# A decoder layer on one core: the delta rule takes q unnormalised, its decay differences come from rows spread by DMA, and the tile order is chosen anew

## The chip, the cores and the metric

The kernel runs on one core of one Trainium2 chip. TensorE (PE) multiplies, VectorE (DVE), ScalarE (ACT) and GpSimd (POOL) do the elementwise work, and the SyncE queue (SP) issues every DMA. The metric is the device time of one execution in microseconds, as the median of three runs. All data are float32. A projection is computed as three products of "hi" and "lo" halves, so each of its K-steps is three matmuls.

## What is computed

The layer mixes 512 tokens of width 1024 by three branches (differential attention, gated DeltaNet, cross-attention into 256 memory tokens), merges them by gates, and ends with a squared-ReLU MLP. The change is in the DeltaNet branch. Cut to that:

```python
q = chunk(l2norm(q.astype(f32)) * dk ** -0.5)
k = chunk(l2norm(k.astype(f32)))
G = jnp.cumsum(g, axis=-1)
decay = jnp.exp(jnp.where(causal, G[..., :, None] - G[..., None, :], -jnp.inf))
lower = jnp.where(strict, jnp.einsum('bhnid,bhnjd->bhnij', k_beta, k) * decay, 0.0)
sol = lax.linalg.triangular_solve(lower + jnp.eye(C), rhs, left_side=True, lower=True, unit_diagonal=True)
intra = jnp.where(causal, jnp.einsum('bhnid,bhnjd->bhnij', q, k) * decay, 0.0)
q_dec = q * jnp.exp(G)[..., None]
...
v_new = u_c - jnp.einsum('bhcd,bhde->bhce', w_c, state)
o = jnp.einsum('bhcd,bhde->bhce', qd, state) + jnp.einsum('bhij,bhje->bhie', a_c, v_new)
...
y_b = rms_norm(o_dn, dn_norm_g) * jax.nn.silu(dn_z)
```

The output of each head is RMS-normalised over its 128 values, so a factor common to a whole row of o (that of q's own norm) falls out, except for the epsilon that is added under the root.

## The kernel before

Work is cut into weight tiles of 128 output columns. A mixing tile takes its weights from a 512 KB load (`w_raw`, three buffers), ACT rounds them to `w_hi`, DVE makes `w_lo`, and PE runs 8 K-steps of three matmuls into one of two accumulator banks (`main_part`, L1749 to L1751: 24 matmuls of 512 columns, or of 256 for the 16 memory tiles `mk` and `mv`). ACT then empties the bank (`evacuate`). PE may start tile t once the evacuation of tile t-2 is done. There are 104 mixing tiles; after them come the branch, output and MLP tiles, which the change leaves alone.

Between pieces of these tiles PE runs two other chains, each a list of steps that use one PSUM area: attention (`ps_a`) and the delta rule (`ps_d`). The delta rule handles the 8 heads in 4 pairs; one pair is 8 blocks of 128 x 128 (2 heads x 4 chunks of 128 tokens). The steps of a pair, in PE's order: `dv`, `dk`, `dq` transpose the convolved v, k, q to rows of tokens; `dE` multiplies a masked copy of the decays (made on POOL in `ET`) by a triangle of ones, and ACT turns the product into `ET = exp(differences)`; `dkT`, `dkb` transpose k and beta k; `dL` forms the triangular matrix; `T1` and the steps `Za`, `Wb`, `Z5`, `W5`, `Zl`, `Wl` invert it in 32 x 32 pieces; `dqT` and `dqd` transpose the normalised q, without and with its decay; `dA` forms q k^T; `dU`, `dW` and the chunk steps `sa`, `sb` run the recurrence; `dO` transposes the result. Behind `dq` DVE squares, sums, takes a root and scales q (`scale_by_norm`, L1493 to L1501).

The order on every engine is not written out: `plan_order` places each step when its inputs are due, from a table of durations, over the tile sequence `ORDER`. Each engine's queue is then strictly in order, SP's too. `decay` (PE L1925, ACT L1180) makes the exponentials of the running decays once, for all heads, and signals `g_exp`. SP's queue also carries the three steps of the attention bias (`bias`): step 1 (L833) spreads 8 rows to a 1.5 MB scratch tensor, `bias_rows`, step 2 (L837) reads `strip` from it. A gate tile is evacuated into the single buffer `gate_st`, halved and shifted on POOL (L960), and stored by SP (L853); the evacuation of the next gate tile waits until that store has landed (`g_out`, L1091).

## Time and profile before

| | |
|---|---|
| median of 3 runs | 1385.65 us (1385.17 to 1386.16) |
| the profiled execution | 1388.61 us, of which the span from its first to its last instruction is 1386.8 us |
| granted PE clock, mean | 0.994 |
| PE, DVE, ACT, POOL busy | 1363.1, 775.9, 483.7, 190.3 us |
| mixing tiles | until 819.8 us |
| matmuls on PE in the trace | 10588 |

The page gives the busy time of each engine, the chain of work that ended last, and groups of instructions with their mean duration and the idle time before them. Matmuls are pipelined: the duration of one (0.39 us for 512 columns) is longer than the distance to the next one's start (0.23 us). What a matmul costs PE is therefore read from starts in the timeline.

### The profile page before, as it was taken

How to read it: one execution, taken by the hardware profiler on the slowest of the kernel's cores; microseconds unless marked ns; L12 is line 12 of the kernel's file. 1: busy time of each engine (PE TensorE's matmuls, PEld its weight loads, DVE VectorE, ACT ScalarE, POOL GpSimd, SP SyncE). 2: the span in 40 equal slices, each digit the busy share in tenths (PEclk: the TensorE clock that was granted, in tenths of full speed). 3: DMA queues.
4: the chain of work that ended last, by engine and by line, in shares of the span. 5: the costliest groups of instructions: out<-in, count | busy, mean ns of one | idle time of the engine just before them, and what ended most of it. 6: DMA issues, size and time to landing. Idle time of an engine off the chain costs nothing.

```text
span 1386.8 us, 24640 instructions
## 1 busy us (share of the span) xinstructions
PE 1363.1 (98%) x10588; PEld 1133.9 (82%) x10588; DVE 775.9 (56%) x1281; ACT 483.7 (35%) x782; POOL 190.3 (14%) x138
## 2 busy tenths in 40 slices
PE   8999999999999999999999999999989999999998
PEld 8689887887888877887888888888988888888886
DVE  6796327844865957769554534554366522355332
ACT  5244433433534434444334221113533212222220
POOL 1112000020000200002101232232202200022010
PEclk9999999999999999999999999999999999999998
DMA  5144322212123222222222466644323323232221
GB/s 213 61 175 139 109 69 91 81 65 78 55 76 99 81 66 63 77 87 89 70 66 96 148 209 195 185 145 154 125 66 119 92 93 102 94 92 91 91 61 61
DMA packets 46435, 143.15 MB, mean 103 GB/s; under 512 B 4944, under 2 KB 7416, under 8 KB 46328
## 3 DMA queue, kind: packets, MB, share of 16 engines
q1 hardware_dynamic: 46328, 141.59, 31.9%
q8 instruction: 84, 1.38, 0.4%
q14 instruction: 23, 0.19, 0.0%
HBM read 126.88 MB, written 16.27 MB: 103 GB/s over the span
## 4 chain that ended last, share of the span: by engine, by line
PE 89%; DVE 7%; ACT 1%; issue 1%; DMA 1%; SPq 0%; DVEq 0%; ACTq 0%
PE acc L1749 24%; PE acc L1751 23%; PE acc L1750 23%; PE ps_d L1903 2%; PE ps_a L1824 2%; PE ps_a L1835 1%; PE ps_d L1865 1%; DVE w_lo L1314 1%; DVE conv_y L1416 1%; PE ps_a L1814 1%; PE ps_a L1803 1%; PE ps_d L1875 1%; PE ps_d L1879 1%; PE ps_d L1881 1%; PE ps_a L1830 1%
## 5 line engine op out<-in xcount | busy, mean ns | idle before, releaser
L1749 PE MATMUL acc<-n_hi,w_hi 128*128 128x512 f32 (+1 forms) x888 | 356.4, 401 | 2.0 <-ACT conv_x L1085 1.4
L1751 PE MATMUL acc<-n_hi,w_lo 128*128 128x512 f32 (+1 forms) x888 | 343.2, 386 | 0.0
L1750 PE MATMUL acc<-n_lo,w_hi 128*128 128x512 f32 (+1 forms) x888 | 342.7, 386 | 0.0
L1013 ACT CAST w_hi<-w_raw 128x1024 fp32r<-128x1024 f32 x172 | 180.4, 1049 | 386.8 <-PE acc L1751 386.2
L1314 DVE TENSOR_TENSOR w_lo<-w_raw,w_hi 128x1024 fp32r<-128x1024 f32 x172 | 237.3, 1384 | 117.0 <-ACT w_hi L1013 116.2
L1749 PEld LDWEIGHTS acc<-n_hi,w_hi 128*128 128x128 f32 x888 | 167.3, 188 | 37.8 <-issue 4.6
L1751 PEld LDWEIGHTS acc<-n_hi,w_lo 128*128 128x128 f32 x888 | 167.1, 188 | 36.3
L1750 PEld LDWEIGHTS acc<-n_lo,w_hi 128*128 128x128 f32 x888 | 167.6, 189 | 30.8 <-issue 0.5
L960 POOL TENSOR_SCALAR gate_st<-gate_st 128x512 f32<-128x512 f32 x24 | 24.7, 1028 | 468.5 <-ACT gate_st L1092 468.4
L1751 PE MATMUL acc<-y_hi,w_lo 128*128 128x512 f32 x192 | 76.0, 396 | 0.0
L1749 PE MATMUL acc<-y_hi,w_hi 128*128 128x512 f32 x192 | 76.0, 396 | 0.0
L1750 PE MATMUL acc<-y_lo,w_hi 128*128 128x512 f32 x192 | 76.0, 396 | 0.0
L1001 POOL TENSOR_TENSOR h_lo<-sq,h_hi 128x512 fp32r<-128x512 f32 x32 | 41.4, 1292 | 239.9 <-DVE h_hi L1671 239.9
L1259 ACT ACTIVATE sq<-relu 128x512 f32<-128x512 f32 x32 | 20.2, 632 | 123.6 <-DVE relu L1669 123.6
L1749 PE MATMUL acc<-h_hi,w_hi 128*128 128x512 f32 x152 | 60.0, 395 | 0.0
L1750 PE MATMUL acc<-h_lo,w_hi 128*128 128x512 f32 x152 | 60.0, 395 | 0.0
L1751 PE MATMUL acc<-h_hi,w_lo 128*128 128x512 f32 x152 | 60.0, 395 | 0.0
L1416 DVE SCALAR_TENSOR_TENSOR conv_y<-conv_x,par,conv_y 128x512 f32<-128x512 f32 x72 | 57.4, 797 | 2.6
L1314 DVE TENSOR_TENSOR wx_lo<-w_raw,wx_hi 128x1024 fp32r<-128x1024 f32 x28 | 45.5, 1636 | 11.5 <-ACT wx_hi L1013 11.5
L1013 ACT CAST wx_hi<-w_raw 128x1024 fp32r<-128x1024 f32 x28 | 29.2, 1041 | 45.5 <-PE acc L1751 45.1
L1751 PEld LDWEIGHTS acc<-y_hi,w_lo 128*128 128x128 f32 x192 | 36.2, 188 | 8.7
L1750 PEld LDWEIGHTS acc<-y_lo,w_hi 128*128 128x128 f32 x192 | 36.2, 188 | 8.7
(359 smaller groups left out, 2339.8 us busy)
## 6 DMA issues: line engine op xcount, KB each, us to landing
w_raw<-weights SPq DMA_DIRECT2D x200, 512.0 KB, 3.7
gate_scratch<-gate_st SPq DMA_DIRECT2D x24, 256.0 KB, 2.8
g_in<-gate_scratch SPq DMA_DIRECT2D x24, 256.0 KB, 4.0
y_raw<-y_scratch SPq DMA_DIRECT2D x16, 256.0 KB, 3.8
x_tok<-x SPq DMA_DIRECT2D x4, 512.0 KB, 5.5
y_scratch<-y_st SPq DMA_DIRECT2D x4, 512.0 KB, 3.0
y_scratch<-d_ET SPq DMA_DIRECT2D x4, 512.0 KB, 3.8
y_scratch<-y_st SPq DMA_DIRECT2D x8, 256.0 KB, 2.5
```

Of the source, the lines that this page charges most:

```text
L960: nc.gpsimd.tensor_scalar(gate_st[:], gate_st[:], 0.5, 0.5, ALU.mult, ALU.add).then_inc(gs_ready, 1)
L1001: nc.gpsimd.tensor_tensor(h_lo[:, f % 16], sq[:, f % 2], h_hi[:, f % 16].bitcast(F32), ALU.subtract).then_inc(hl_ok, 1)
L1013: nc.scalar.copy(hi_of_tile(t), w_raw[:, t % RAW]).then_inc(hi_ready, 1)
L1259: nc.scalar.activation(sq[:, f % 2], relu[:, f % 2], ACT.Square).then_inc(sq_ok, 1)
L1314: V_.tensor_tensor(lo_of_tile(t), w_raw[:, t % RAW], hi_of_tile(t).bitcast(F32), ALU.subtract).then_inc(lo_ready, 1)
L1416: ins = V_.scalar_tensor_tensor(out=y, in0=conv_x[:, n % 2, j:j + S], scalar=par[:, col + j:col + j + 1], in1=y, op0=ALU.mult, op1=ALU.add)
L1749: mm(bank, wh, hi_of(k), start=start and k == 0, stop=False)
L1750: mm(bank, wh, lo_of(k), start=False, stop=False)
L1751: last = mm(bank, wl, hi_of(k), start=False, stop=stop and k == KT - 1)
L1803: last = mm(ps_a[:, s // 2, (s % 2) * MEM:(s % 2 + 1) * MEM], cq_T[:, h % 2, dt, s * P:(s + 1) * P], mk_T[:, 2 * h + dt], start=dt == 0, s ...
L1824: last = mm(ps[:, col:col + (q + 1) * P], qkv_T[rows_m, h % 2, 0, q * P:(q + 1) * P], qkv_T[rows_m, h % 2, 1, 0:(q + 1) * P], start=True, ...
L1903: last = mm(dst[m], a[:, m], b[:, m], start=True, stop=True)
```

## The change

1. **Raw q.** `dq` still transposes q, but ACT writes only its squares (`U`), and copies the convolved q as it is to `QT`, which needs no transposition. DVE sums the squares to `q_eps`, the epsilon for the output's norm. The norm of q, `dqT` and `dqd` go, on PE, ACT and DVE. The decay that was multiplied into q is now multiplied into the product: in `sb` the product of q and the state goes to a bank of its own, and DVE adds it, scaled, to what ACT has copied (two instructions for each chunk but the first, which wait for ACT).
2. **Spread rows.** `decay` gets a fourth product, the running decays as 32 rows, which ACT copies into `ET`; it also writes the running decays over `gdec`. SP stores the rows (`store_rows`, 16 KB) and reads them back for each pair into all 128 partitions (`spread_rows`, 512 KB as 1024 pieces of 512 bytes). POOL subtracts where it multiplied. ACT, within `dq`, waits for POOL and applies Relu and Exp. `dE` goes from PE.
3. **Tile order.** `ORDER` is another, and all engines' orders follow from it and from the changed table of durations.

```diff
@@ plan
-ORDER = [("conv", 0), ("z", 0), ("gate", 1), ("mem", 0), ("cq", 0), ("gate", 1), ("cq", 1), ("conv", 1),
...
+ORDER = [("conv", 0), ("gate", 2), ("z", 0), ("mem", 0), ("cq", 0), ("cq", 1), ("conv", 1), ("cq", 2),
...
-        out += [(k, p, 0) for k in ("dv", "dk", "dq", "dE", "dkT", "dkb", "dL", "T1", "dqT", "dA", "dqd")]
+        out += [(k, p, 0) for k in ("dv", "dk", "dq", "dkT", "dkb", "dL", "T1", "dA")]
...
+    add("SP", "rows", ("rows_out", 0), 0.1, [("AT", 2)])
+    for p in range(HB // 2):
+        add("SP", "rows", ("rows", p), 0.1, [("OUT", "yb", d_idx[("dO", p - 1, 0)]) if p else ("OUT", "rows_out", 0)])
@@ sync
+            def store_rows(n):
+
+                sp.wait_ge(g_exp, 1)
+                sp.dma_start(row_dram, ET[0:HB * ST, 0]).then_inc(rows_out, 16)
+
+            def spread_rows(p):
+
+                if p:
+                    sp.wait_ge(yb_out, 16 * p)
+                else:
+                    sp.wait_ge(rows_out, 16)
+                sp.dma_start(ET[:], bass.AP(tensor=row_dram.tensor, offset=row_dram.offset + 8 * p * row_dram.ap[0][0],
+                                            ap=[[0, P], [row_dram.ap[0][0], 8], [1, P]])).then_inc(rows_in, 16)
@@ gpsimd
-                    if p:
-                        pool.wait_ge(yb_out, 16 * p)
-                    last = nc.gpsimd.tensor_tensor(ET[:], over(cst[:, C_AFTER, :], 8),
-                                                   along(flat(gdec[:, heads]), P), ALU.mult)
+                    pool.wait_ge(rows_in, 16 * (p + 1))
+                    last = nc.gpsimd.tensor_tensor(ET[:], along(flat(gdec[:, heads]), P), ET[:], ALU.subtract)
@@ scalar
-                if kind == "dE":
-                    last = nc.scalar.activation(flat(ET[:]), two(ps_d), ACT.Exp)
+                if kind == "dq":
+                    nc.scalar.activation(flat(U[:]), two(ps_d), ACT.Square)
+                    nc.scalar.copy(flat(QT[:]), conv_o[:, 0].rearrange("p a s -> p (a s)"))
+                    act.wait_ge(d_pool, dP[d_idx[("dk", p, 0)] + 1])
+                    nc.scalar.activation(flat(ET[:]), flat(ET[:]), ACT.Relu).then_inc(ach, 1)
+                    act.wait_ge(ach, p + 1)
+                    last = nc.scalar.activation(flat(ET[:]), flat(ET[:]), ACT.Exp, scale=-1.0)
...
+                nc.scalar.copy(flat(gdec[:]), ps_d[:, 2, 0:32])
+                nc.scalar.copy(ET[0:HB * ST, 0], ps_d[0:HB * ST, 2, P:2 * P]).then_inc(g_exp, 1)
@@ vector
-                    last = scale_by_norm(Q, 1.0, 4 * EPS, P ** -0.5)
+                    dve.wait_ge(g_exp, 1)
+                    link(V_.reduce_sum(q_eps, U[:], AX_X))
+                    last = V_.tensor_scalar(q_eps, q_eps, 4 * EPS, EPS * P, ALU.add, ALU.mult)
...
-                elif kind == "dqT":
-                    dve.wait_ge(g_exp, 1)
-                    last = V_.tensor_tensor(Q[:], Q[:], along(flat(e_in[:, heads]), P), ALU.mult)
...
+                    dve.wait_ge(d_act, dA[i + 1])
+                    if c:
+                        for hh in range(2):
+                            last = V_.scalar_tensor_tensor(out=O[:, 4 * hh + c], in0=ps_d[:, 2, hh * P:(hh + 1) * P],
+                                                           scalar=e_in[:, 2 * p + hh, c:c + 1], in1=O[:, 4 * hh + c],
+                                                           op0=ALU.mult, op1=ALU.add)
@@ tensor
-                elif kind in ("dqT", "dqd", "dkT", "dkb", "dO"):
-                    src = {"dqT": Q, "dqd": Q, "dkT": K, "dkb": KB, "dO": O}[kind]
+                elif kind in ("dkT", "dkb", "dO"):
+                    src = {"dkT": K, "dkb": KB, "dO": O}[kind]
...
-                elif kind == "dE":
-                    for m in range(8):
-                        last = mm(dst[m], ET[:, m], cst[:, C_UPTO, :], start=True, stop=True)
...
-                            mm(o_ps, QDT[:, 4 * hh + c], state[:, hh], start=True, stop=False)
-                        mm(o_ps, AT[:, 4 * hh + c], vn, start=c == 0, stop=True)
+                            mm(ps_d[:, 2, hh * P:(hh + 1) * P], QT[:, 4 * hh + c], state[:, hh], start=True, stop=True)
+                        mm(o_ps, AT[:, 4 * hh + c], vn, start=True, stop=True)
...
+                mm(ps_d[0:HB * ST, 2, P:2 * P], flat(gdec[:]), cst[:, C_UPTO, :], start=True, stop=True).then_inc(g_mm, 1)
```

The first place is PE where pair 0 enters its inversion: `dqd` (L1865 on `d_Q`) ahead of the first `Za` (L1875). Before:

```order
L1751 MATMUL acc<-m_hi,w_lo 128x256
L1865 MATMUL ps_d<-cst,d_Q 128x128 x8
L1875 MATMUL ps_d<-d_TT,d_SCR 32x32 x32
L1749 MATMUL acc<-m_hi,w_hi 128x256
L1750 MATMUL acc<-m_lo,w_hi 128x256
```

The same place now (L1901 is `Za`, L1780 to L1782 are the tile's products):

```order
L1782 MATMUL acc<-m_hi,w_lo 128x256
L1901 MATMUL ps_d<-d_TT,d_SCR 32x32 x32
L1780 MATMUL acc<-m_hi,w_hi 128x256
L1781 MATMUL acc<-m_lo,w_hi 128x256
```

The eight transpositions are gone and nothing stands in their place; the same holds for `dqT` and `dE`, in each of the four pairs.

The second place is SP's queue from the last load ahead of the spread bias to the load of `strip`. Before (L833 is `bias` step 1, L837 step 2, L853 the store of the first gate tile):

```order
L815 DMA w_raw<-weights 128x1024 x4
L833 DMA bias_rows<-bias_scratch 1024x1x384
L815 DMA w_raw<-weights 128x1024 x3
L837 DMA strip<-bias_rows 128x8x256
L853 DMA gate_scratch<-gate_st 128x512
L815 DMA w_raw<-weights 128x1024 x20
```

Now (L881 stores the rows, L889 spreads those of pair 0, L840 is `bias` step 1, L860 stores the gate tiles 6 and 7, L844 is `bias` step 2):

```order
L822 DMA w_raw<-weights 128x1024 x4
L881 DMA y_scratch<-d_ET 32x128
L889 DMA d_ET<-y_scratch 128x8x128
L840 DMA bias_rows<-bias_scratch 1024x1x384
L822 DMA w_raw<-weights 128x1024
L860 DMA gate_scratch<-gate_st 128x512
L822 DMA w_raw<-weights 128x1024
L860 DMA gate_scratch<-gate_st 128x512
L822 DMA w_raw<-weights 128x1024
L844 DMA strip<-bias_rows 128x8x256
```

The 1.5 MB transfer now stands behind two row transfers, and ahead of the first gate tile's store, with one load between.

The third place is ACT's queue over the same time. Before, from the copy of k (L1173, step `dk`) to that of q (step `dq`):

```order
L1173 COPY d_K<-ps_d 128x1024
L1099 ACTIVATE conv_x<-conv_y 128x512
L1106 ACTIVATE z_t<-zs 128x512
L1013 CAST w_hi<-w_raw 128x1024
L1087 COPY zs<-acc 128x512
L1013 CAST w_hi<-w_raw 128x1024
L1092 ACTIVATE gate_st<-acc 128x512
L1013 CAST w_hi<-w_raw 128x1024
L1068 COPY mk_T<-acc 128x256
L1173 COPY d_Q<-ps_d 128x1024
```

Now, from the first gate tile's evacuation (L1112) to the end of `dq` (L1171 to L1176) and the next tile's:

```order
L1112 ACTIVATE gate_st<-acc 128x512
L1198 COPY d_K<-ps_d 128x1024
L1119 ACTIVATE conv_x<-conv_y 128x512
L1033 CAST w_hi<-w_raw 128x1024
L1112 ACTIVATE gate_st<-acc 128x512
L1033 CAST w_hi<-w_raw 128x1024
L1107 COPY zs<-acc 128x512
L1126 ACTIVATE z_t<-zs 128x512
L1171 ACTIVATE d_U<-ps_d 128x1024
L1172 COPY d_QT<-conv_o 128x1024
L1174 ACTIVATE d_ET<-d_ET 128x1024
L1176 ACTIVATE d_ET<-d_ET 128x1024
```

The second gate tile (tile 7) is evacuated here, ahead of the casts and copies of the tiles behind it, where before there was one gate tile in this stretch; and `dq` is four full passes in a row.

## Rows read from the trace of the kernel before

**Rows 1.** The page, busy time, share of the span and instructions of each engine.

```profile
PE 1363.1 (98%) x10588; PEld 1133.9 (82%) x10588; DVE 775.9 (56%) x1281; ACT 483.7 (35%) x782; POOL 190.3 (14%) x138
PE 89%; DVE 7%; ACT 1%; issue 1%; DMA 1%; SPq 0%; DVEq 0%; ACTq 0%
```

**Rows 2.** PE by stretch: stretch in us, its length, PE busy (instructions), clock, DMA.

```profile
40.00:100.00 60.00, 55.37 (x285) 1.00 0.36 122
100.00:820.00 720.00, 717.82 (x7408) 1.00 0.29 90
```

**Rows 3.** Waits of PE: who waited for whom, us in total, times, longest.

```profile
PE ps_d L1879 <- issue: 1.5, 1, 1.5
PE acc L1749 <- ACT conv_x L1085: 1.4, 1, 1.4
PE ps_d L1860 <- DVE conv_o L1430: 1.2, 1, 1.2
PE ps_d L1860 <- DVE d_V L1518: 0.7, 1, 0.7
PE ps_d L1875 <- DVE d_KBT L1525: 0.6, 1, 0.6
```

**Rows 4.** Timeline of PE at `dE` of pair 1: start us, us, instruction.

```profile
273.56 1.95 PE L1868 MATMUL ps_d<-cst,d_ET 128*128 128x128 f32 x16
275.26 0.48 PE L1749 MATMUL acc<-n_hi,w_hi 128*128 128x512 f32 x1
275.58 0.39 PE L1750 MATMUL acc<-n_lo,w_hi 128*128 128x512 f32 x1
275.81 0.39 PE L1751 MATMUL acc<-n_hi,w_lo 128*128 128x512 f32 x1
```

**Rows 5.** Timeline of PE at `dqT` of pair 0.

```profile
119.64 1.03 PE L1865 MATMUL ps_d<-cst,d_Q 128*128 128x128 f32 x8
120.43 0.36 PE L1749 MATMUL acc<-m_hi,w_hi 128*128 128x256 f32 x1
120.63 0.28 PE L1750 MATMUL acc<-m_lo,w_hi 128*128 128x256 f32 x1
```

**Rows 6.** Timeline of ACT at `decay`, start us, us, instruction.

```profile
75.90 0.20 ACT L1180 ACTIVATE e_all<-ps_d 128x32 f32<-128x32 f32 x1
```

**Rows 7.** Timeline of SP: issues of the bias, loads and the first gate store.

```profile
72.82 0.75 SPq L833 DMA_DIRECT2D bias_rows<-bias_scratch  x1
83.33 9.94 SPq L815 DMA_DIRECT2D w_raw<-weights  x3
93.79 0.58 SPq L853 DMA_DIRECT2D gate_scratch<-gate_st  x1
```

**Rows 8.** DMA from 74 to 86 us: GB/s moved, in 40 equal slices of 0.3 us.

```profile
GB/s 259 259 341 273 217 188 189 205 195 205 205 205 195 195 200 200 205 205 200 200 205 205 200 195 195 205 200 205 205 195 184 118 15 0 55 96 191 273 382 423
```

**Rows 9.** DMA issues from 60 to 100 us: KB each, median us to landing.

```profile
strip<-bias_rows SPq DMA_DIRECT2D x1, 1024.0 KB, 6.2
gate_scratch<-gate_st SPq DMA_DIRECT2D x1, 256.0 KB, 6.4
```

**Rows 10.** Landing times of all gate stores and reloads, then of all weight loads.

```profile
DMA to landing us min/median/max: 2.0/3.9/6.4
DMA to landing us min/median/max: 3.3/3.7/12.1
```

**Rows 11.** Timeline of PE where tile 9 begins, and at `dO` of pair 3.

```profile
89.85 0.28 PE L1749 MATMUL acc<-m_hi,w_hi 128*128 128x256 f32 x1
...
791.02 1.03 PE L1865 MATMUL ps_d<-cst,d_LT 128*128 128x128 f32 x8
...
819.77 0.40 PE L1749 MATMUL acc<-y_hi,w_hi 128*128 128x512 f32 x1
```

**Rows 12.** Groups of DVE and ACT: form xcount, busy us, mean ns.

```profile
L1549 DVE SCALAR_TENSOR_TENSOR state<-state,e_all,ps_d 128x128 f32<-128x128 f32 x24 | 7.2, 343 | 11.8 <-PE ps_d L1916 11.6
L1173 ACT COPY d_Q<-ps_d 128x1024 f32<-128x1024 f32 x8 | 8.1, 1016 | 20.2 <-PE ps_d L1903 13.1 <-PE ps_d L1860 7.1
```

More of the change, by code:

```diff
@@ L124, in vector_before @@
     kind, p, c = step
-    return {"dq": ("dv", p, 0), "dE": ("dv", p, 0), "dkT": ("dk", p, 0), "dkb": ("dk", p, 0), "dL": ("dk", p, 0),
-            "T1": ("dL", p, 0), "dqT": ("dL", p, 0), "dA": ("dL", p, 0), "dqd": ("dqT", p, 0)}.get(kind)
+    return {"dq": ("dv", p, 0), "dkT": ("dk", p, 0), "dkb": ("dk", p, 0), "dL": ("dk", p, 0),
+            "T1": ("dL", p, 0), "dA": ("dL", p, 0)}.get(kind)
 def scalar_before(step):
@@ L257, in plan_order @@
                 add("ACT", "fin", ("fin", t), 0.65, [("DVE", "conv", t)])
-                add("DVE", "fin", ("fin", t), 0.75, [("ACT", "fin", t)] + ([("PE", "delta", d_idx[free])] if free else []))
+                add("DVE", "fin", ("fin", t), 0.75, [("ACT", "fin", t)] + ([("ACT" if tiles[t][0] == "dq" else "PE", "delta", d_idx[free])]
+                                                                  if free else []))
             else:
@@ L273, in plan_order @@
             deps.append(("POOL", "delta", d_idx[pool_before(s)]))
-        if kind == "dqd":
-            deps.append(("DVE", "at", p))
         if kind in ("dq", "dk", "dv"):
@@ L280, in plan_order @@
         if "A" in PARTS[kind]:
-            add("ACT", "delta", ("delta", i), ACT_US.get(kind, 1.05), [mm, ("DVE", "delta", i) if kind == "dL" else ("POOL", "delta", d_idx[("dA", p, 0)]) if kind == "W5" else None])
+            add("ACT", "delta", ("delta", i), ACT_US.get(kind, 1.05), [mm, ("DVE", "delta", i) if kind == "dL" else ("POOL", "delta", d_idx[("dA", p, 0)]) if kind == "W5" else
+                                                                ("POOL", "delta", d_idx[("dk", p, 0)]) if kind == "dq" else None])
         if "D" in PARTS[kind]:
@@ L295, in plan_order @@
                 deps.append(("DVE", "at", p))
-            if kind == "dk" and p:
-                deps.append(("OUT", "yb", d_idx[("dO", p - 1, 0)]))
+            if kind == "dk":
+                deps.append(("OUT", "rows", p))
             add("POOL", "delta", ("delta", i), POOL_US[kind], deps)
@@ L333, in plan_order @@
             "DVE": ("lo", "delta", "attn", "conv", "fin", "finz", "pre"), "POOL": ("delta", "gate", "pre"),
-            "SP": ("load", "gate", "y", "yb", "bias", "pre")}
-    landing = {"load": 3.7, "gate": 2.4, "y": 3.4, "yb": 3.4, "pre": 3.8, "bias": 0.0, "load_gate": 3.8}
+            "SP": ("load", "gate", "y", "yb", "rows", "bias", "pre")}
+    landing = {"load": 3.7, "gate": 2.4, "y": 3.4, "yb": 3.4, "pre": 3.8, "bias": 0.0, "load_gate": 3.8, "rows_out": 2.4, "rows": 4.5}
     order = {e: [] for e in rank}
@@ L498, in build @@
         sd_ = sb_in(dl)
-        names = ["Q", "SCR", "K", "KB", "V", "QT", "QDT", "KTT", "KBT", "ET", "LT", "AT", "TT"]
+        names = ["U", "SCR", "K", "KB", "V", "TF", "QT", "KTT", "KBT", "ET", "LT", "AT", "TT"]
         B = {n: sd_("d_" + n, [P, 8, P]) for n in names}
-        Q, SCR, K, KB, V, QT, QDT, KTT, KBT, ET, LT, AT, TT = (B[n] for n in names)
-        TF, U, WT, O = QT, Q, SCR, LT
+        U, SCR, K, KB, V, TF, QT, KTT, KBT, ET, LT, AT, TT = (B[n] for n in names)
+        WT, O = SCR, LT
         HP = (slice(0, P // 2), slice(P // 2, P))
@@ L628, in build @@
         g_exp = sem("g_exp")
+        rows_out = sem("rows_out")
+        rows_in = sem("rows_in")
         f_mm = sem("f_mm")
@@ L879, in _ @@
             sp_work = {"load": load, "bias": bias, "gate": store_gate, "y": store_attn, "yb": store_delta,
+                       "rows_out": store_rows, "rows": spread_rows,
                        "pre": reload, "load_gate": load_gate}
@@ L1171, in delta @@
                 else:
-                    dst = {"dq": Q, "dk": K, "dqT": QT, "dqd": QDT, "dkT": KTT, "dkb": KBT, "dU": U, "dW": WT}[kind]
+                    dst = {"dk": K, "dkT": KTT, "dkb": KBT, "dU": U, "dW": WT}[kind]
                     last = nc.scalar.copy(flat(dst[:]), two(ps_d))
@@ L1179, in decay @@
                 for m, dst in enumerate((e_in, e_tail, e_all)):
-                    last = nc.scalar.activation(flat(dst[:]), ps_d[:, 2, m * 32:(m + 1) * 32], ACT.Exp)
-                last.then_inc(g_exp, 1)
+                    nc.scalar.activation(flat(dst[:]), ps_d[:, 2, m * 32:(m + 1) * 32], ACT.Exp)
+                nc.scalar.copy(flat(gdec[:]), ps_d[:, 2, 0:32])
+                nc.scalar.copy(ET[0:HB * ST, 0], ps_d[0:HB * ST, 2, P:2 * P]).then_inc(g_exp, 1)
             def ba_copy():
@@ L1853, in delta @@
                     pe.wait_ge(d_pool, dP[d_idx[pool_before(DELTA[i])] + 1])
-                if kind == "dqd":
-                    pe.wait_ge(at_ready, p + 1)
                 dst = [ps_d[:, m // 4, (m % 4) * P:(m % 4 + 1) * P] for m in range(8)]
```

37 lines of the change are left out of this document (19 added, 18 removed), and 2 rows, old and new, of the table PARTS.

## The prediction

> **What bounds the kernel now.** I read the busy shares and the chain of waits first: PE is busy for 98% of the span and holds 89% of the chain that ended last, while DVE is busy for 56%, ACT for 35%, POOL for 14% [rows 1]. PE by stretch comes next. From 100 us to 820 us, where the delta rule and the attention run between pieces of the weight tiles, PE stands idle for 2.2 of 720 us; from 40 us to 100 us for 4.6 of 60 [rows 2]. Its granted clock is full (1.00) in both. So the mixing stage is a queue of PE work without holes, and its length is the sum of what stands in that queue. The delta chain itself does not set the end: its last step, `dO` of pair 3, starts at 791.0 us, and gate tiles fill PE until 819.8 us [rows 11]. What a removed matmul saves is therefore its own time on PE, and a changed wait costs only what it leaves PE idle. The waits of PE in this stage are five short ones, 0.6 to 1.5 us [rows 3].
>
> **What PE loses.** `dE`: its 16 instructions take from 273.56 to 275.26 us, 1.70 us, and the tile's first matmul behind them needs 0.32 us to the next start where 0.23 us is usual, so 1.79 us a pair [rows 4], 7.2 us for four. `dqT`: 0.79 us, and 0.20 us against 0.12 us behind it, 0.87 us a pair [rows 5], 3.5 us for four. `dqd` is the same eight transpositions; it stands right ahead of `Za`, which keeps the restart, so 0.79 us a pair, 3.2 us for four. `decay` gains one product of 128 columns, an eighth of a `dE`: 0.2 us. In `sb` the product with the state goes to its own bank; the number and shape of matmuls stay the same. PE's work falls by 7.2 + 3.5 + 3.2 - 0.2 = **13.7 us**.
>
> **What the other engines gain and lose; it costs nothing as long as PE's queue covers it.** ACT did four passes of 128 x 1024 a pair for these steps (q, ET, QT, QDT), each about 1.02 us [rows 12], and now does four others (Square, copy, Relu, Exp), but in one row, 4.2 us at the same pace with casts counted a little dearer. They are hidden by what PE has queued between `dq` and the next step of its chain, `dkT`: the least is in pair 0, 12 matmuls of 512 columns and 24 of 256, 12 x 0.23 + 24 x 0.12 = 5.6 us. Without that cover it would be up to 4.2 us a pair. Behind these passes on ACT are queued the casts and the evacuations; an evacuation has a whole tile, 5.6 us, before PE needs its bank, so a delay of 4.2 us leaves it in time, just. DVE loses q's norm and `dqT` and gains six small instructions a pair in `sb` of about 0.34 us [rows 12], 2.1 us; DVE is not the bound, so I count nothing. The small ones lengthen each chunk step by about 0.7 us and a wait for ACT's copy; between chunk steps PE has at least one tile part, 1.4 us and often several, and the chain ends some 38 us before the stage does (in the new order seven gate tiles of 5.6 us stand behind `dO`'s place, less a part), where it had 28.7 us. So again nothing.
>
> **The spread rows of pairs 1 to 3.** SP issues them when the output store of the pair before has landed, 3 to 4 us behind its issue. They need an estimated 5 us, POOL 2 us. From `dO` of pair 2 to `dq` of pair 3 there is the shortest distance, about 18 us of PE queue, against 1 + 1.3 + 3.8 + 5 + 2 = 13 us. SP is blocked for those 4 us; a weight load is issued some three tiles ahead, so this is covered as well. I take 0, and up to 2 us for pair 3.
>
> **The first rows and what queues behind them.** This is where I expect a loss. The rows can leave when `decay` is through on ACT. Its third exponential ends at 75.90 + 0.20 = 76.1 us [rows 6], held by the convolution's work ahead of it in ACT's queue. Two small copies bring it to 76.4 us. The store needs at least 2.0 us, the shortest landing of any gate store [rows 10]; I take 2.3 us, so the spread is issued at 78.7 us, and the 1.5 MB bias transfer behind it at 79.5 us instead of 72.8 us [rows 7]. In the trace that transfer moves some 200 GB/s from 75.2 us to 83.5 us [rows 8], so it is done 10.7 us after its issue. Now this is 90.2 us, and 2 us more for the spread's own data ahead of it (512 KB more make a landing 2.5 us later: strip's 6.2 us [rows 9] against 3.7 us of a load [rows 10]): 92.2 us. A load and then the first gate tile's store are issued behind it at about 83.5 us, when `w_lo` of tile 8 is done [rows 7]. In the trace the gate store issued half a microsecond behind `strip` took 6.4 us to land, against 2.0 us at best, and landed 0.7 us after it [rows 9, 10]: it waited its turn. So I let both wait for the bias transfer: load 1.5 us, store 0.7 us, receipt 0.6 us, landed at 95.0 us. Tile 7 is a gate tile too, and its evacuation waits for that landing: it ends at about 95.7 us. PE may not start tile 9 before, and would reach it at 89.85 us, where tile 9 starts now [rows 11]. That is a stall of 5.9 us. It swallows the 1.2 us that PE waits ahead of `dq` for `conv_o` [rows 3], which is long written by then. Net **+4.7 us**; its bounds are 0 (nothing waits its turn) and some 10 us (the spread's 1024 small pieces are as slow as the bias's, 130 a microsecond, and more of the tail is late). I take 4.7 because the gate store behind `strip` is the nearest row.
>
> The Trainium skill (DMA: Bandwidth & Descriptors, Queues, rings and completion order) says that each DMA engine consumes its descriptors in ring order; the trace's 6.4 us behind `strip` agrees. The same page (Specifications) gives 512 bytes as the least size for full rate, and the spread's pieces are of exactly that; by it the spread's data would take about 1 us less and the time be 1375.6 us. No row here shows pieces of 512 bytes.
>
> **Sum.** Span 1386.8 - 13.7 + 4.7 = 1377.8 us. The profiled execution took 1388.61 us, 3.0 us over the median of the runs; I apply the difference, -9.0 us, to the median: 1385.65 - 9.0 = 1376.65, say **1376.6 us**. The waits of 1.5 us (L1879) and 0.6 us (L1875) in the trace [rows 3] may go or come again elsewhere; that is +-2 us.
>
> **Rivals.**
> - *No early stall.* The bias transfer and the store do not hold each other up, or the spread leaves earlier. For it: the transfer's 200 GB/s are only half of what the loads around it reach (up to 423 GB/s in the same row [rows 8]), so not all DMA engines are in it. Against it: a store lands when its last piece does, on whichever engine. Time: 1385.65 - 13.7 = 1372.0 us. Chance 0.22.
> - *The delta chain takes more back.* The spread runs at the bias's pace (1024 pieces, 8 us), which moves the gate store to about 100 us and makes the early stall 9.5 us net, and the four passes of `dq` hold evacuations late by 1 us or so in some pairs. Time 1381 to 1383 us. Chance 0.10; with still more waits of the kind the gain is gone (1383 to 1388 us), 0.06.
> - *Slower than before.* One mechanism: the row spread lands late. ACT waits for it in the middle of `dq`, with casts and evacuations queued behind, so PE runs out of banks one tile later. It decides from the point where the spread takes more than its cover: 18 - 8 = 10 us in pair 3. A load once took 12.1 us to land [rows 10]. For a loss the four pairs must give back over 13.7 us, that is the early stall of 10 us and more than 4 us in pair 3, a spread of 14 us or longer. Nothing in the trace has 512 KB so slow except that one load. Time 1389 us and up. Chance 0.05.
> - *It does not remove what it says.* The new order could put as many switches between the tile pieces as before; but the rows of the order show the steps gone, so I give it nothing of its own.
>
> **How the numbers follow.** The forecast has 0.57. The range reaches from the rival without a stall, less 1.5 us for waits that vanish, to the middle of the second rival: **1370.5 to 1382 us**. A measurement of this kernel tells 0.2% (2.8 us) from no change. Faster by more than that: 0.57 + 0.22 + 0.10 = 0.89; within it 0.06; slower 0.05.
>
> **What would show it right or wrong.** PE's instructions fall by 128 (64 of `dE`, 64 transpositions) and rise by 2, and the branch tiles start near 811 us instead of 819.8 us. A wait of PE on ACT's evacuation of the first or second gate tile, of 4 to 7 us, stands near 90 us, and ahead of it on ACT one for the DMA of the gate store; that store lands over 9 us after its issue. The wait for `conv_o` at `dq` of pair 0 is gone. PE's idle time between 100 us and the end of mixing stays under 5 us. If the early wait is missing, the time is 1372 us; if PE shows waits for ACT behind `dq` in every pair, the cover was counted too large; if `dO` of pair 3 ends within a few microseconds of the first branch tile, the chain has become the bound.

## The result

The changed kernel takes **1393.05 us** (median of 4 runs, 1391.91 to 1395.57) against 1385.91 us of before (4 runs): ratio 1.0054, 95% interval 1.0041 to 1.0066. It is 7 us slower, where I forecast 9 us faster.

The profiled execution took 1391.91 us, its span is 1390.1 us; the branch tiles start at 824.4 us, 4.6 us later than before [rows 11], where 811 us was forecast. The page shows that the work did go (compare [rows 1]):

```profile
PE 1351.9 (97%) x10462; PEld 1122.1 (81%) x10462; DVE 755.6 (54%) x1246; ACT 482.9 (35%) x784; POOL 190.4 (14%) x138
```

PE has 126 instructions fewer and is busy 11.2 us less. PE by stretch (us, PE busy, granted clock, DMA share, GB/s), the same two as in [rows 2] and then four short ones:

```profile
40.00:100.00 60.00, 46.92 (x210) 0.95 0.32 95
100.00:820.00 720.00, 712.01 (x7334) 0.99 0.30 94
90.00:102.00 12.00, 0.00 (x0) 0.64 0.71 242
102.00:104.00 2.00, 1.45 (x4) 0.50 0.09 34
104.00:106.00 2.00, 2.00 (x6) 0.50 0.53 144
106.00:108.00 2.00, 2.00 (x10) 0.73 0.92 342
```

From 90 us to 102 us PE does nothing at all. PE's waits, which answer to [rows 3], name the releaser, and two kinds of wait inside the 32 x 32 steps (L1905, L1907) have grown:

```profile
PE acc L1780 <- ACT gate_st L1112: 12.7, 1, 12.7
PE ps_d L1907 <- issue: 3.4, 2, 2.4
...
PE ps_d L1905 <- issue: 1.0, 1, 1.0
```

The timeline of PE shows both ends of the long wait, and that matmuls behind it start 0.43 us apart instead of 0.23 us, at a granted clock of 0.50 (1.2 GHz of 2.4):

```profile
89.46 0.40 PE L1782 MATMUL acc<-n_hi,w_lo 128*128 128x512 f32 x1
102.55 0.77 PE L1780 MATMUL acc<-n_hi,w_hi 128*128 128x512 f32 x1 [12.69 <-ACT gate_st L1112]
103.12 0.63 PE L1781 MATMUL acc<-n_lo,w_hi 128*128 128x512 f32 x1
103.54 0.63 PE L1782 MATMUL acc<-n_hi,w_lo 128*128 128x512 f32 x1
```

ACT in turn waited for the DMA that stores the first gate tile:

```profile
101.81 0.60 ACT L1112 ACTIVATE gate_st<-acc 128x512 f32<-128x512 f32 x1 [16.39 <-DMA gate_scratch<-gate_st]
```

SP's queue over this time (start us, us) is the line to read most closely; it answers to [rows 7]:

```profile
76.18 0.33 SPq L881 DMA_DIRECT2D y_scratch<-d_ET  x1
77.59 0.38 SPq L889 DMA_DIRECT2D d_ET<-y_scratch  x1
78.01 0.76 SPq L840 DMA_DIRECT2D bias_rows<-bias_scratch  x1
81.71 10.84 SPq L822 DMA_DIRECT2D w_raw<-weights  x1
92.59 0.44 SPq L860 DMA_DIRECT2D gate_scratch<-gate_st  x1
```

The issue of one weight load, normally 0.33 us, held SP for 10.84 us, so the gate store behind it was not even issued before 92.59 us; it then took 9.2 us to land. The DMA from 76 us to 104 us shows what stood ahead of both: the GB/s moved, in 40 slices of 0.7 us, and the spread of pair 0 with its us from issue to landing.

```profile
GB/s 0 23 0 12 44 45 45 46 43 46 41 34 47 43 47 43 33 31 27 42 82 184 192 204 244 204 197 280 396 399 424 344 231 203 214 202 146 53 0 44
...
d_ET<-y_scratch SPq DMA_DIRECT2D x1, 512.0 KB, 14.2
```

The rows crawl at 45 GB/s until 90 us; only then does the bias transfer run at its 200 GB/s, and the store behind it lands at 101.8 us. Over all four pairs the median landing is 12.4 us.

From 40 us to the first branch tile, with distances between starts summed by kind of step in both traces: `dE`, `dqT` and `dqd` took 14.0 us before, nothing now. Against that, idle time between 40 us and 110 us rose from 4.6 to 15.6 us, issue waits behind 110 us from 1.5 to 4.9 us, the matmuls of the weight tiles from 545.2 to 548.6 us (most of it at the half clock), the delta rule's other matmuls by 1.9 us, 0.4 us of it in `decay`. After the mixing stage the profiled span is 1.3 us shorter.

### The profile page after: what moved, and what is told of

Read it like the earlier page. It is cut to its first block, busy times and chain, and to the rows that moved or that the text cites. A ratio compares the mean times of both kernels' runs of the same rounds, so it can differ in the third digit from the quotient of the medians.

```text
span 1390.1 us, 24344 instructions
## 1 busy us (share of the span) xinstructions
PE 1351.9 (97%) x10462; PEld 1122.1 (81%) x10462; DVE 755.6 (54%) x1246; ACT 482.9 (35%) x784; POOL 190.4 (14%) x138
## 3 DMA queue, kind: packets, MB, share of 16 engines
q8 instruction: 83, 1.36, 0.4%
## 4 chain that ended last, share of the span: by engine, by line
PE 90%; DVE 5%; issue 2%; ACT 2%; DMA 1%; SPq 0%; DVEq 0%; ACTq 0%
PE acc L1780 25%; PE acc L1782 24%; PE acc L1781 24%; PE ps_d L1929 2%; PE ps_a L1855 2%; PE ps_a L1866 1%; PE ps_a L1845 1%; PE ps_a L1834 1%; PE ps_d L1901 1%; DVE conv_y L1443 1%; PE ps_d L1905 1%; PE ps_d L1894 1%; DVE w_lo L1340 1%; PE ps_d L1907 1%; DMA gate_scratch<-gate_st 1%
## 5 line engine op out<-in xcount | busy, mean ns | idle before, releaser
L1780 PE MATMUL acc<-n_hi,w_hi 128*128 128x512 f32 (+1 forms) x888 | 357.2, 402 | 14.6 <-ACT gate_st L1112 12.7
L1782 PE MATMUL acc<-n_hi,w_lo 128*128 128x512 f32 (+1 forms) x888 | 343.9, 387 | 0.0
L1780 PEld LDWEIGHTS acc<-n_hi,w_hi 128*128 128x128 f32 x888 | 167.9, 189 | 51.7 <-issue 18.3
L1782 PEld LDWEIGHTS acc<-n_hi,w_lo 128*128 128x128 f32 x888 | 167.6, 189 | 36.4
L1782 PE MATMUL acc<-y_hi,w_lo 128*128 128x512 f32 x192 | 76.0, 396 | 0.0
L1780 PE MATMUL acc<-y_hi,w_hi 128*128 128x512 f32 x192 | 76.0, 396 | 0.0
L1780 PE MATMUL acc<-h_hi,w_hi 128*128 128x512 f32 x152 | 60.0, 395 | 0.0
L1782 PE MATMUL acc<-h_hi,w_lo 128*128 128x512 f32 x152 | 60.0, 395 | 0.0
L956 POOL TENSOR_TENSOR d_ET<-gdec,d_ET 128x1024 f32<-128x1024 f32 x4 | 8.6, 2147 | 297.7 <-DMA d_ET<-y_scratch 165.4
L1780 PEld LDWEIGHTS acc<-y_hi,w_hi 128*128 128x128 f32 x192 | 36.2, 188 | 8.7
## 6 DMA issues: line engine op xcount, KB each, us to landing
d_ET<-y_scratch SPq DMA_DIRECT2D x4, 512.0 KB, 12.4
```

The source lines that it names most:

```text
L1780: mm(bank, wh, hi_of(k), start=start and k == 0, stop=False)
L1782: last = mm(bank, wl, hi_of(k), start=False, stop=stop and k == KT - 1)
```

## Experiments: the three parts of the change

**The tile order alone**, in before:

```diff
-ORDER = [("conv", 0), ("z", 0), ("gate", 1), ("mem", 0), ("cq", 0), ("gate", 1), ("cq", 1), ("conv", 1),
+ORDER = [("conv", 0), ("gate", 2), ("z", 0), ("mem", 0), ("cq", 0), ("cq", 1), ("conv", 1), ("cq", 2),
...
```

> The kernel before with the new tile order alone: nothing of the delta rule is changed, and no rows are spread. Theory A (the loss comes from the first gate tile's store queued behind the row spread and the bias transfer): without the spread the bias transfer is issued near 73 us and done by 84 us, so the store lands in time, no wait over 2 us near 90 us, and the time is that of the kernel before, 1383 to 1388 us. Theory B (the new tile order is bad in itself, with two gate tiles in a row that share one buffer): a wait of PE over 8 us near 90 us here too, and 1398 us or more.

Measured: 1404.61 us, ratio 1.0129 [1.0110, 1.0149]. There is no long wait near 90 us (1.2 us for the gate tile), so two gate tiles in a row do not make the stall. The new cost lies in the first branch tiles (PE's waits):

```profile
PE acc L1749 <- POOL y_lo L954: 7.2, 4, 2.6
...
PE ps_d L1885 <- DVE d_TT L1534: 2.1, 1, 2.1
```

It is not the delta chain that ends late here: its last output is stored at 788.88 us, in before at 793.40 us. It is attention. SP's timeline at the store of its last head (L862):

```profile
812.20 0.32 SPq L862 DMA_DIRECT2D y_scratch<-y_st  x1
```

In before this store stands at 777.58 us and in the changed kernel at 778.41 us. The reloads of these outputs are issued from 814.64 us on (in before from 781.88 us), and POOL makes its first `y_lo` at 819.28 us instead of 790.20 us. With the steps of before, the new order lets attention end some 34 us later. Order and steps belong together; the order is not a part with a price of its own.

**The other two parts with before's order:**

```diff
@@ the changed kernel
-ORDER = (new)
+ORDER = (that of before)
```

> The changed kernel with the tile order of before: raw q and the spread rows stay. Theory A: only one gate tile stands early and its store has nothing waiting behind it, so the stall near 90 us is gone with the slow-clock stretch behind it; PE's work is 13.7 us less than before: 1372 us, at most 1377 us with short waits. Theory C (the loss is ACT's row of four passes in dq and its wait for POOL, in every pair): the time stays above 1385 us whatever the tile order.

Measured: 1387.91 us, 1.0010 [1.0000, 1.0021]. Here it is a weight load that stands behind the slow transfers. On ACT:

```profile
101.23 1.04 ACT L1033 CAST w_hi<-w_raw 128x1024 fp32r<-128x1024 f32 x1 [15.79 <-DMA w_raw<-weights]
```

PE waits 9.8 us at the same place. So a stall comes with the slow transfer in either tile order. With the new order the stall is about 3 us and the whole kernel some 5 us longer.

**Raw q alone**, before's order, `dE` kept, no spread:

```diff
@@ before
-        out += [(k, p, 0) for k in ("dv", "dk", "dq", "dE", "dkT", "dkb", "dL", "T1", "dqT", "dA", "dqd")]
+        out += [(k, p, 0) for k in ("dv", "dk", "dq", "dE", "dkT", "dkb", "dL", "T1", "dA")]
...
```

> Raw q alone on the kernel before, in its tile order: the norm of q and both its transpositions are gone, the decay differences are still made by products (dE) and no rows are spread. PE has 64 transpositions less, 3.5 + 3.2 = 6.7 us of its time by the prediction's terms, and nothing new is queued on the DMA rings: 1379 us if the mixing stage gives it all back, 1376 to 1382 us with the waits of PE inside the 32 x 32 steps going up or down by 3 us. If raw q costs something itself (the longer chunk steps, ACT's Square), 1384 us or more.

Measured: 1384.32 us, 0.9988 [0.9978, 0.9997], a gain of 1.9 us where PE's work falls by 6.7 us. Between 110 us and 815 us its PE shows two waits that before does not have or has shorter:

```profile
PE ps_d L1903 <- issue: 2.5, 4, 1.2
PE ps_d L1909 <- DVE d_TT L1555: 2.1, 1, 2.1
```

In that profile the branch tiles start at 815.8 us, 3.9 us earlier than in before's. The two waits cost 3.1 us more than the issue wait there, which is about the rest of the 6.7 us. The median shows only half of these 3.9 us, and code that is merely moved may change a time by some microseconds (last section of experiments), so 1.9 us is no safe price for raw q.

**Spread rows alone**, before's order, q normalised and transposed as before, the rows read in one piece (next section):

```diff
@@ before
+                if kind == "dq":
+                    nc.scalar.copy(flat(Q[:]), two(ps_d))
+                    act.wait_ge(d_pool, dP[d_idx[("dk", p, 0)] + 1])
+                    nc.scalar.activation(flat(ET[:]), flat(ET[:]), ACT.Relu).then_inc(ach, 1)
...
-                elif kind == "dE":
-                    for m in range(8):
-                        last = mm(dst[m], ET[:, m], cst[:, C_UPTO, :], start=True, stop=True)
```

> Before, with one part of the change alone: the decay differences from spread rows (read as one piece of 4 KB); q is still normalised and transposed twice, the order is before's. Theory additive: PE loses dE, 7.2 us, gains 0.2 us, no stall near 90 us: 1386.2 - 7.0 = 1379.2 us, and raw q is worth little beyond it (1379.0 us was measured with both). By the PE work alone raw q should add 6.7 us: then this kernel comes out at 1386 - (7.1 - 1.9 ...) i.e. near 1381 to 1384 us, and the two parts sum to the 7 us measured together (raw q alone gave 1.9 us).

Measured: 1388.81 us (1384.16 to 1392.02), 1.0019 [1.0005, 1.0033]. Both expectations fail: `dE` is gone from PE, and the kernel is slower. DVE's timeline in pair 0 shows a part of it:

```profile
97.78 1.23 DVE L1520 TENSOR_TENSOR d_SCR<-d_Q 128x1024 f32<-128x1024 f32 x1 [1.22 <-ACT d_ET L1175]
...
101.12 1.89 DVE L1329 SCALAR_TENSOR_TENSOR smd<-smd 128x8 f32<-128x8 f32 x1
...
105.79 5.19 DVE L1339 TENSOR_TENSOR w_lo<-w_raw,w_hi 128x1024 fp32r<-128x1024 f32 x3
```

DVE's norm of q now waits for ACT's two extra passes, and one of its small instructions takes 1.89 us instead of 0.17 us, from 101.12 us to 103.01 us; POOL's multiply of `d_K` (L958) runs from 101.08 us to 102.98 us. `w_lo`, queued behind on DVE, starts 2.8 us later than before, and PE waits for it (4.0 us). Its issue waits are 3.0 us longer than those of before. These 7.0 us use up what `dE` gave; the profiled span is 2.1 us over before's, and the rest is not taken apart. With raw q the norm is not there. Together the two parts gain 7 us (below), alone one gains 1.9 us and the other loses 3.3 us; that raw q is what makes room for the ACT passes fits the trace of pair 0, but no run shows it by itself.

## Experiments: why the spread is slow

**One piece instead of eight.** The rows in a tensor of their own, so that a pair's 8 rows are 4 KB in a row:

```diff
-    row_dram = y_dram[1, 0:HB * ST, KT - 1, 0:P]
+    row_dram = rows_dram
...
-                sp.dma_start(ET[:], bass.AP(tensor=row_dram.tensor, offset=row_dram.offset + 8 * p * row_dram.ap[0][0],
-                                            ap=[[0, P], [row_dram.ap[0][0], 8], [1, P]])).then_inc(rows_in, 16)
+                sp.dma_start(flat(ET[:]), bass.AP(tensor=row_dram.tensor, offset=row_dram.offset + 8 * p * P,
+                                                  ap=[[0, P], [1, 8 * P]])).then_inc(rows_in, 16)
```

> The changed kernel, its 32 rows of running decays stored side by side in a tensor of their own, so that a pair's 8 rows are read as 128 pieces of 4 KB instead of 1024 pieces of 512 bytes; all else as in the changed kernel. Theory A: the spread lands after about 4 us instead of 10 to 14 us, the first gate store some 8 us earlier, and PE's wait near 90 us falls from 12.7 us to 4 to 6 us: about 1381 us, since the slow-clock stretch gets shorter too. If the spread's length does not matter, the time stays at 1393 us.

**The same 1024 pieces of 512 bytes, but near each other** (rows 768 bytes apart; only the tensor changes):

> As the run before this one, but with rows 768 bytes apart, so that they stay 1024 pieces of 512 bytes, all within 6 KB of memory instead of 16 KB apart from row to row. It tells why the spread is slow. If the number of pieces is what costs, it lands after 10 to 14 us as in the changed kernel, and the time is 1393 us. If the distance of 16 KB between the rows is what costs, it lands after 5 us and the time is that of the run with 4 KB pieces.

Measured: 1382.13 us (0.9971 [0.9952, 0.9990]) and 1380.50 us (0.9957 [0.9939, 0.9975]). The spread lands in 4.0 us and 4.1 us. So neither the number nor the size of the pieces is the cause, but where the rows lie. Three further kernels change only the distance of the rows, each in a tensor of its own like the kernel with 768 bytes:

```diff
-    rows_dram = nc.dram_tensor("row_scratch", (HB * ST, 3 * P // 2), F32, kind="Internal").ap()
+    rows_dram = nc.dram_tensor("row_scratch", (HB * ST, 4224), F32, kind="Internal").ap()
```

(1024 and 2048 in the other two; the expectations call the 768 bytes above 512 by mistake.)

> The changed kernel, with the eight rows of a pair 16,896 bytes apart in a scratch tensor of their own instead of 16,384; still 1024 pieces of 512 bytes. Rows 16 KB apart landed in 14.2 us (pair 0) and 10.5 us, rows 512 bytes apart in 4.0 us. Theory alignment: the eight rows a power of two apart fall on the same part of the memory; at 16.5 KB the spread lands in about 4 us, PE's wait near 90 us is 4 us or less, the time 1380 us. Rival distance: any rows this far apart are slow; landing 10 us or more, wait 12 us, 1393 us.

> The changed kernel with the eight rows of a pair 4096 bytes apart in a scratch tensor of their own; still 1024 pieces of 512 bytes. Rows 16,384 bytes apart landed in 10.4 to 14.2 us, rows 512 or 16,896 bytes apart in 3.6 to 4.0 us. Theory alignment, by the row's low address bits: 4096 is as bad as 16,384 if what counts is a part of the memory picked by address bits under 4096; then landing 10 us or more. If the bits that matter lie above, the landing is between, 4 to 8 us.

> The same with rows 8192 bytes apart. Theory alignment: as slow as 16,384 (10 us or more), or halfway (6 to 8 us) if two parts of the memory take turns at this distance. Rival: only 16,384 is slow; then 4 us.

| rows apart, bytes | landing, pair 0, us | median of four | load's issue holds SP, us | PE waits for `gate_st`, us | time, us |
|---|---|---|---|---|---|
| one piece of 4 KB | 4.0 | 3.9 | 0.34 | 1.9 | 1382.13 |
| 768 | 4.1 | 4.0 | 1.91 | 3.9 | 1380.50 |
| 4,096 | 10.2 | 9.6 | 5.55 | 7.2 | 1385.24 (1 run) |
| 8,192 | 16.7 | 16.1 | 12.91 | 14.5 | 1398.24 (1 run) |
| 16,384 (the change) | 14.2 | 12.4 | 10.84 | 12.7 | 1393.05 |
| 16,896 | 3.6 | 3.8 | 0.74 | 2.4 | 1383.83 (1 run) |

Rows 16,384 bytes apart are slow and rows 16,896 bytes apart are as fast as any, so it is not that they lie far apart. The three slow distances are powers of two from 4 KB up, and also multiples of 4 KB: no run has rows 12 KB apart, which would tell the two apart. The kernels with 4,096, 8,192 and 16,896 bytes stand on one execution each; their landings, of four pairs each, are far apart, but their times may be off by 3 us and more (the eight runs with 768 bytes lie between 1376.2 and 1386.5 us). The landings of pair 0 as the view of DMA issues has them, first with rows 8,192 bytes apart:

```profile
d_ET<-row_scratch SPq DMA_DIRECT2D x1, 512.0 KB, 16.7
```

and with rows 16,896 bytes apart:

```profile
d_ET<-row_scratch SPq DMA_DIRECT2D x1, 512.0 KB, 3.6
```

The Trainium skill (DMA: Bandwidth & Descriptors, Latency and other measured facts) reports the same kind of loss for HBM rows 2 MiB and more apart, cured by a small pad, and infers that the streams fall on the same memory channel. Here it shows at 4 KB already, and a pad of 512 bytes cures it at 16 KB; no run here shows which part of the memory collides.

At 8 KB there is a second stall, in pair 3. It is the mechanism of my slower rival, at its place. POOL's timeline, waiting for the rows:

```profile
643.17 1.90 POOL L956 TENSOR_TENSOR d_ET<-gdec,d_ET 128x1024 f32<-128x1024 f32 x1 [16.23 <-DMA d_ET<-row_scratch]
```

and PE's, waiting for ACT's passes behind it:

```profile
647.30 1.97 PE L1894 MATMUL ps_d<-cst,d_K 128*128 128x128 f32 x8 [4.28 <-ACT d_ET L1176]
```

In the changed kernel the same rows reach POOL at 637.32 us, ACT waits 2.59 us in the middle of `dq`, and PE waits for nothing: its cover was enough for a landing in 10.4 us, and some 4 us short for one in 15.7 us.

**The order of the two transfers**, bias spread ahead of the rows, once with rows 16 KB apart and once with one piece:

```diff
+    order["SP"].remove(("bias", 1))
+    order["SP"].insert(order["SP"].index(("rows_out", 0)), ("bias", 1))
```

> The changed kernel with one transfer moved: the spread of the bias rows (1.5 MB) is issued ahead of the store and the spread of the decay rows, at 73 us as in the kernel before, instead of behind them. If the first gate store waits for all that is queued ahead of it (theory A), the bias is done by 84 us, the decay spread (slow, 9 to 11 us) by 93 to 95 us, and PE's wait near 90 us shrinks from 12.7 us to about 6 us: 1385 us. If only the bias transfer mattered and the spread runs beside it, the wait is gone: 1380 us or less. If the order of the two is indifferent (the sum of both must pass in any case), 12 us stay and the time is 1393 us.

> The changed kernel with both: rows side by side in a tensor of their own (128 pieces of 4 KB) and the bias transfer ahead. By theory A nothing long is left in front of the first gate store: the wait of PE near 90 us is under 1 us, so 1.9 us less than with the 4 KB pieces alone, 1380 us. The short waits of PE inside its 32 x 32 steps (put down to issue, 8 us with the 4 KB pieces) decide the rest: theory D says that they come from where PE's instruction stream is fetched and stay at 4 to 9 us.

Measured: 1393.40 us, as slow as the changed kernel, with a wait of 13.2 us for the gate store; and 1378.84 us (0.9950 [0.9933, 0.9967]), with one of 1.6 us. The slow spread costs the same on either side of the bias transfer, since the store stands behind both. The first of these kernels also tells what the hold of SP is worth. Its SP issues the gate store at 85.17 us, 7.4 us earlier than the changed kernel does:

```profile
85.17 2.12 SPq L862 DMA_DIRECT2D gate_scratch<-gate_st  x1
```

The view of DMA issues has its us to landing:

```profile
gate_scratch<-gate_st SPq DMA_DIRECT2D x1, 256.0 KB, 17.2
```

So the store lands at 102.4 us, no earlier than in the changed kernel (101.8 us). What delays the store is the transfers ahead of it; the late issue alone doesn't account for it.

**One piece with before's order, and that with the bias ahead:**

> The changed kernel with the tile order of before and the rows side by side (4 KB pieces). With the old order PE stood 9.8 us near 93 us, because a weight load issued at 81 us behind the slow spread and the bias transfer landed only at 101 us. Theory A: with the fast spread that load lands by 94 us and ACT's cast is 7 us earlier: the wait falls to 1 to 3 us and the time to 1379 us. If the load was late for another reason, it stays at 1388 us.

> Raw q and spread rows, before's tile order, the eight rows of a pair read as one piece of 4 KB, and the spread bias transfer ahead of the row store. Theory: the early stall is gone as in both kernels with rows in one piece (1379.0 and 1378.8 us), PE's work is 13.7 us less than before; what is left are waits inside the 32 x 32 steps: 1376 to 1379 us, the same as either within 1 us, since each edit alone already removes the stall. Rival: the order of the two transfers matters by itself (it took 3.3 us from the kernel with the new order); then 1376 us or less.

Measured: 1379.03 us (0.9954 [0.9940, 0.9969]) and 1378.83 us (0.9952 [0.9934, 0.9970]). With the stall gone, the four kernels with raw q and rows in one piece stand between 1378.8 and 1382.1 us. Between the two tile orders lie 3 us with the bias behind the rows and nothing with it ahead. Moved code alone may make a difference of that size (next section), so no price of the order can be read from them.

## Experiments: the issue waits in the 32 x 32 steps

PE's waits called issue behind 110 us are 1.5 us in before, 4.9 us in the changed kernel and 8.3 us in the one with 4 KB rows. The longest there ends at 130.72 us, and in that stretch (127.5 to 131.5 us, DMA by queue: packets, MB, share) one block of instructions is moved, 16 KB by the page's total of 83 blocks and 1.36 MB in the changed kernel:

```profile
q8 instruction: 1, 0.02, 1.4%
```

The block moves at 128.0 to 128.25 us and PE waits on until 130.72 us, so it is no proof that PE waited for code. In before nine such blocks are moved between 120 us and 163 us, one every four to eight microseconds, and PE waits for none. The Trainium skill (Runtime: NRT & Kernel Launch, Instruction fetch mechanics) says that code comes in blocks of 16 KiB and that the fetch is mostly hidden. The size agrees with the trace, and so does the hiding in before; whether it fails at the waits is what the next runs were to tell. Ten matmuls without effect, put into a wait of 2.4 us at the start, move all later code by some 40 places. They went into the 4 KB kernel, before, and the changed kernel:

```diff
                 transpose_rows(j)
+                if j == 1:
+                    keep_awake(10)
```

> The kernel with rows in one piece (1382.1 us), with ten more matmuls of the kind that keep PE awake, put into a wait of 2.4 us at the start of the kernel. The data path is the same; every later PE instruction moves by some 40 places in PE's code. That kernel's PE showed 8.3 us of waits called issue inside the steps of 32 x 32 matmuls, before shows 1.5 us. Theory code position: these waits are PE's own code arriving late, so they depend on where the steps lie in the code; they change by 2 us or more in sum or move to other steps, and the time changes with them (1378 to 1386 us). Rival dependency: the waits come from the steps' own data (a releaser that the profile doesn't name); then the same steps wait as long as before, 8 us in sum, and the time stays within 1 us of 1382.1 us.

> Before, with the same ten matmuls put into the same wait at the start; every later PE instruction moves by some 40 places in PE's code, nothing else changes. Before's PE showed 1.5 us of issue waits between 110 us and 815 us, less than any other kernel (2.5 to 8.3 us). Theory code position: before is well placed, and a shift gives it some of the waits of the others: 2 to 6 us in sum, at other steps, time 1386 to 1390 us. Rival dependency (the waits come from what the change does to the steps' data): still 1.5 us at the same step, and the time within 1 us of 1385.5 us.

> The changed kernel, with the same ten matmuls put into the same wait at the start. It showed 4.8 us of issue waits between 110 us and 815 us. Theory code position: their sum or their places change (1 to 7 us), the wait for the gate tile's evacuation near 90 us stays at 12 to 13 us, and the time comes out between 1390 and 1396 us. Rival dependency: 4.8 us at the same places, the time within 1 us of 1393 us.

Measured: 1378.09 us (0.9938 [0.9919, 0.9957]) instead of 1382.13 us (the intervals of the two ratios overlap slightly, and the profiled spans are only 1.2 us apart), 1386.30 us (1.0008 [0.9999, 1.0017]) and 1391.74 us (1.0051 [1.0034, 1.0068]). The shifted 4 KB kernel has 3.5 us of these waits instead of 8.3 us, and they stand at other steps: the one of 2.9 us is gone, one of 1.3 us has come at 338 us. Before, shifted, has 0.5 us, at a weight tile:

```profile
PE acc L1753 <- issue: 0.5, 1, 0.5
```

and the shifted changed kernel 3.3 us. So the places of these waits follow the position in the code, and the rival that the steps' own data hold them falls. The sum does not follow the code alone. Eight kernels have exactly the PE program of the changed kernel: the changed kernel itself, the five with another layout of the rows, and the two with the bias ahead in the new order. Their waits recur at the same steps (the first, of 2.4 to 2.9 us, in seven of the eight), but they sum up to between 4.2 us and 8.3 us; moving nothing but SP's bias transfer took the 8.3 us of the 4 KB kernel down to 4.2 us. So the fall to 3.5 us above cannot be put down to the shift. The theory that before was merely well placed finds no support either: its two placements have 1.5 us and 0.5 us, all other kernels 2.5 to 8.3 us. That the removed steps had given the fetch time to run ahead doesn't fit either, since before's own steps in the new order have 3.7 us, and those with only `dE` gone 4.4 us. What sets the sum stays open, and that PE waits for code is argued from the places, not shown. Each sum is that of one profiled execution; how much it varies between executions of one kernel is not known.

## Why the prediction was wrong, step by step

- **What bounds the kernel: right.** Mixing is PE's queue, and PE's holes decide.
- **What PE loses: right.** 13.9 us less the product in `decay` was forecast; the traces differ by 14.0 us in these steps, and by 126 instructions.
- **ACT's four passes, DVE, cover: right.** The passes take 108.56 to 112.57 us, 4.0 us against 4.2 us, and no PE wait behind `dq` appears in any pair. The wait for `conv_o` is gone. The later spreads cost PE nothing, though they landed in 10.4 to 15.6 us where I had 5 us. That the cover held is in part luck: in pair 3 it was 10.4 us, just over the 10 us that I gave as the cover, and 15.7 us with rows 8 KB apart used it up.
- **The failed step: the landing of the first rows.** In the sum the spread's own data ahead of the bias transfer have "2 us more", read off `strip` and a load, whose pieces lie otherwise, and a whole landing is "an estimated 5 us", for which no row is named. It took 14.2 us. With rows that land in 4 us and all else as in the change (one piece, 768 or 16,896 bytes apart) the kernel is 1.7 to 4.9 us faster than before instead of 7.1 us slower: the slow landing costs 9 to 12 us, and it alone turns the gain into a loss. The upper bound I named, the bias's pace of 130 pieces a microsecond, was no bound either: 1024 pieces in 12 us are 85 a microsecond. Where the rows lie in memory I never read as a quantity, though it follows from the tensor that the change puts them in (rows of 8 x 512 values of 4 bytes).
- **What queues behind: the right places, the wrong instant.** The wait of PE on ACT's gate evacuation behind the gate store was forecast at 5.9 us and measured at 12.7 us. I had the store issued at 83.5 us and waiting its turn in the transfers; in fact SP itself was held for 10.84 us in the issue of the load ahead. The landing is as late where the store is issued at 85.17 us (bias ahead), so the turn in the transfers was the right reading, and their length was not. With rows in 4 us, the wait is 1.9 us to 3.9 us, less than my 5.9 us. The rival with 1024 pieces at the bias's pace, 9.5 us net, was the nearest in the stall and had a chance of 0.10; it fell short of the 11.0 us net that idle time grew by. By its time (1389 us and up) the rival that came was "Slower than before", with 0.05. Its spread of 14 us and its early stall of 10 us came as written; the wait in pair 3, which it named as its mechanism, did not, and the rest of the loss came from what follows.
- **What was missing.** The half clock behind a long wait, which has no term in the sum: the 12.7 us are followed by 4.6 us at 0.50, and an issue wait of 2.4 us by a stretch at 0.58 from 144 us to 148 us. The matmuls of the weight tiles took 3.3 us more in all. And the issue waits, +3.4 us, which I put at +-2 us that "may go or come again".
- **The base.** The profiled execution of before took 3.0 us more than its median, that of the changed kernel 1.1 us less. I carried the 3.0 us over as a constant; 4 us of the miss of 16.4 us is this. The other 12.3 us is the span: 6.3 us of stall, some 5 us of slower matmuls, 3.4 us of issue waits, less 1.3 us in the late stages and about 1 us in attention and elsewhere.
- **The sum without the failed step** can be read from the chip: with raw q and rows that land in 4 us the kernels measure 1378.1 to 1383.8 us, above the forecast of 1376.6 us. Even then only 2 to 7 of the 13.7 us are gained over before. What keeps the rest is only known in part: issue waits of 3.3 to 8.3 us, and a stall of 1.6 to 3.9 us in those with the new order.

## What to carry to other kernels

Before reading a few rows into all partitions, write down the distance between them: if it is 4, 8 or 16 KB (other multiples of 4 KB were not run), lay them side by side or pad them, which here turned 14.2 us into 4 us and a loss of 7 us into a gain of 2 to 5 us (7 us with the bias transfer ahead or before's tile order besides). Ask of a new transfer what is issued behind it in the same queue and who waits for that; a single buffer that must be stored before it is written again passes the delay on to PE. And try the parts of a change singly before giving each a price: raw q alone gained 1.9 us, the spread rows alone (in one piece) lost 3.3 us, the tile order alone lost 19 us, and the first two together gained 7 us.

## What the runs showed of the hardware

- Reading 8 rows of 512 bytes into 128 partitions takes 3.6 to 4.1 us with rows 768 or 16,896 bytes apart, 10.2 us at 4,096, 16.7 us at 8,192 and 14.2 us at 16,384.
- The issue of a DMA held SP while earlier transfers of 1024 pieces each crawled: 10.84 us here, 5.55 us and 12.91 us with rows 4 KB and 8 KB apart, 0.34 us to 1.91 us where the rows land in 4 us. Everything later in the queue is issued late by that. The gate store lands no earlier when it is issued ahead of such a hold (102.4 us against 101.8 us): it is behind the same transfers either way.
- After a wait of 12.7 us PE ran for 4.6 us at the lower of its two clocks. After one of 3.9 us the granted clock was 0.57 over the next 4 us, after one of 3.0 us (the 4 KB kernel with shifted code) 0.58. PE by stretch with rows 768 bytes apart:

```profile
94.00:98.00 4.00, 4.00 (x11) 0.57 0.40 102
```

- After a wait of 1.9 us it did not; the same stretch with rows in one piece has 23 matmuls instead of 11:

```profile
94.00:98.00 4.00, 4.00 (x23) 1.00 0.82 274
```

- A DVE instruction of 0.17 us took 1.89 us (101.12 to 103.01 us) while POOL worked on 128 x 1024 elements (101.08 to 102.98 us), in the kernel with spread rows alone.
